# Loads into one of nine ring slots issued as 112 + 8 + 8 partitions in place of 128

## The chip, the cores and the metric

The kernel runs on one core of one Trainium2 chip. The metric is device time in microseconds of one execution. The kernel before has a median of 1238.89 us over three runs (1235.37 to 1240.13).

## The reference

Two layers of a diffusion backbone on 256 latent tokens of width 1024, with 256 context tokens. Layer 0 mixes with latent attention and a pooling mixer and then applies a dense SwiGLU. Layer 1 mixes with a 2-D Fourier transform and then applies eight expert SwiGLUs, of which each token uses two. All is float32.

```python
def swiglu(h, w1, w3, w2):
    return (jax.nn.silu(h @ w1) * (h @ w3)) @ w2

def moe_swiglu(h, router_w, w1, w3, w2):
    logits = (h @ router_w).astype(jnp.float32)
    top_v, top_i = lax.top_k(logits, TOP_K)          # TOP_K = 2 of N_EXPERTS = 8
    top_p = jax.nn.softmax(top_v, axis=-1)
    gates = jnp.sum(jax.nn.one_hot(top_i, N_EXPERTS, dtype=jnp.float32) * top_p[..., None],
                    axis=-2).astype(h.dtype)
    y = jnp.zeros_like(h)
    for e in range(N_EXPERTS):
        y = y + gates[..., e:e + 1] * swiglu(h, w1[e], w3[e], w2[e])
    return y
```

w1 and w3 are 1024 x 3584 for each expert, w2 is 3584 x 1024: 44 MB an expert, 352 MB for the eight.

## The kernel before, in words

SP issues every load, in one fixed order, on one hardware queue (q1 in the profile). Up to about 400 us of the span this is the modulation, mixer and dense weights. From then on it is the experts' weights, and the change lies there.

An expert's weights are cut into 42 pieces of 1 MB, taken as 21 pairs (PAIRS). A pair is 128 rows, one for each partition, of 16 KB (4096 float32). The pairs go through a ring of nine slots (SLOTS = 9) in SBUF: pair number n goes to slot n % 9, and PAIR_PIECE says where in the tensor "held" a slot lies. Pairs 0 to 19 and the last few come as two halves of 1 MB (comes_by_halves, load_half, L680). All others come whole (load, L676), 143 of them in an execution. Before it issues a load into a slot, SP waits for the semaphore e_used, which TensorE raises as it finishes with pieces: expert_loads holds the rule.

Each slot has its own semaphore, piece_in[slot][0], for whole loads and for first halves. A transfer raises it by 16. TensorE waits for 16 times the number of landings expected there. loads_into(slot, lo, hi) counts the loads of a slot in a range of pair numbers, landings adds them up over experts, and the last pair's count is worked out from the same function beside the final down.

Experts are handled in groups of two (GROUP). Each has room for 96 tokens, those at places 1, 5 and 7 only for 64 (LIGHT_PLACES). The matmuls of w1 and w3 are L2398 ("up", N = 256), those of w2 L2413 ("down", N = 512). The matmuls take longer in an expert with 96 places than in one with 64; the bytes loaded are the same. ScalarE and VectorE turn the products in between (L1099, L1761), the results are summed back over tokens by L2367, and L2377 gathers the tokens of the next group.

A second loop over rounds would serve an expert with more tokens than its places; with these inputs it isn't entered. ACT issues eight small table loads (q10) during the experts. The instruction streams of the engines are themselves fetched from memory by DMA (q8 in the profile).

Of the kernel before, what the change touches and what calls it, by code (L numbers as in the profile page):

```python
# [15 lines left out]
P = 128  # L16
# [100 lines left out]
FIRST_LOOP = UNROLLED * GROUP_PAIRS - 1  # L117
SLOTS = 9
ODD_IN_HALF = {3: 1, 8: 0}
BY_HALVES = PAIRS - 1  # L120
END_HALVES = FIRST_LOOP + GROUP_PAIRS - 4
PAIR_AT = {("up", 0, 0): 0, ("up", 0, 1): 2, ("down", 3): 4, ("up", 1, 0): 5, ("up", 1, 1): 7, ("down", 0): 9,
# [97 lines left out]
def build(nc, vec_d, con_d, rope_d, x_d, ctx_d, ada_d, mixa_d, mixb_d, attn_d, mixout_d, ffn_d,  # L220
          dft_d, fnet_d, router_d, moe_d, out_d):
    ctx = ExitStack()
    with ctx:
# [3 lines left out]
        def sem(name):  # L227
            return ctx.enter_context(nc.semaphore(name))
# [25 lines left out]
        def view(t, at, *dims):  # L254

            n = int(np.prod(dims))
            v = t[:, at:at + n]
            if len(dims) == 2:
                return v.rearrange("p (a b) -> p a b", a=dims[0])
            if len(dims) == 3:  # L260
                return v.rearrange("p (a b c) -> p a b c", a=dims[0], b=dims[1])
            return v
# [91 lines left out]
        unit_free = [sem(f"unit_free{i}") for i in range(UNIT_SLOTS)]  # L354
        piece_in = [[sem(f"piece_in{slot}_{s}") for s in range(1 if slot in ODD_IN_HALF else 2)] for slot in range(SLOTS)]
        scratch_free = sem("scratch_free")
# [47 lines left out]
        half_in, half_free = [sem(f"half_in{n}") for n in range(HALF_BUFFERS)], [sem(f"half_free{n}") for n in range(HALF_BUFFERS)]  # L404
        for slot, b in ODD_IN_HALF.items():
            piece_in[slot].append(half_in[b])
        odd_before = [16 * len(range(ODD_IN_HALF[slot], HALVES, HALF_BUFFERS)) if slot in ODD_IN_HALF else 0 for slot in range(SLOTS)]
        sum_ready, scaled_summed = sem("sum_ready"), sem("scaled_summed")
# [52 lines left out]
        def queue_at(i, q):  # L461

            return PAIRS * i + q - 1 if i or q >= AHEAD else q
# [8 lines left out]

        def loads_into(slot, lo, hi):

            return len([n for n in range(lo, hi) if n % SLOTS == slot])

        def landings(group, j, q):

            slot = slot_of_pair(group, j, q)
            if ahead_of_loop(group):  # L480
                return loads_into(slot, 0, queue_at(GROUP * group + j, q) + 1)
            here = loads_into(slot, FIRST_LOOP, FIRST_LOOP + PAIRS * j + q + 1)
            each = loads_into(slot, FIRST_LOOP, FIRST_LOOP + GROUP_PAIRS)
            return each * group + (loads_into(slot, 0, FIRST_LOOP) - UNROLLED * each + here)

        def comes_by_halves(n):

            return n < BY_HALVES or END_HALVES <= n < FIRST_LOOP + GROUP_PAIRS

# [62 lines left out]
        def landed(slot):  # L552

            return view(held, PAIR_PIECE[slot] * PIECE, 2 * PIECE)
# [77 lines left out]
        def _(sp):  # L632
# [37 lines left out]
            def pair_of(e, q):  # L670

                return moe_d[e, 2 * q:2 * q + 2].rearrange("a (m s) c -> (a m) s c", s=2)

            def load(slot, e, q):

                sp.dma_start(landed(slot).rearrange("p (s c) -> p s c", s=2), pair_of(e, q)).then_inc(piece_in[slot][0], 16)  # L676

            def load_half(slot, e, q, s):

# [47 lines left out]
            def expert_loads(e, before, i, group, j):  # L727

                by_halves = [] if ahead_of_loop(group) else [q for q in range(PAIRS) if comes_by_halves(FIRST_LOOP + PAIRS * j + q)]
                for q in range(PAIRS):  # L730
                    if q == 0 and j == 0 and not isinstance(group, int):
                        sp.wait_ge(e_used, PIECES * i - 2)
                    elif (q + PAIRS - SLOTS) % PAIRS not in QUAD_SECOND:
                        sp.wait_ge(e_used, PIECES * i + used_with((q + PAIRS - SLOTS) % PAIRS, 1, q - SLOTS - 1))
                    if q not in by_halves:
                        load(slot_of_pair(group, j, q), before if q == AHEAD else e, q)
                    elif q in QUAD_SECOND:
                        for s in range(2):
                            for d in (1, 0):
                                load_half(slot_of_pair(group, j, q - d), e, q - d, s)  # L740
                    elif q not in QUAD_FIRST:
                        for s in range(2):
                            load_half(slot_of_pair(group, j, q), e, q, s)
# [3 lines left out]
            for (phase, *_), q in PAIR_AT.items():  # L747
                for s, n in ([(s, queue_at(0, q) + d) for s in range(2) for d in range(2)] if phase == "up" else
                             [(s, queue_at(0, q) + d) for d in range(1 if q == AHEAD else 2) for s in range(2)]):
                    if SLOTS <= n < BY_HALVES and q != AHEAD:  # L750
                        left = n - SLOTS
# [1793 lines left out]
```

## Time and profile before

| | |
|---|---|
| median of three runs | 1238.89 us |
| profiled execution, its own time | 1238.51 us |
| its span | 1236.7 us |
| mean granted TensorE clock | 0.991 |
| TensorE busy | 1194.7 us, 97% |
| read from memory | 456.81 MB, 370 GB/s over the span |
| longest queue, q1 | 455.77 MB |

The span is the time from the first to the last recorded instruction. A DMA share of 1.00 means that all sixteen DMA engines of the core are busy; it can read 1.01, because successive packets overlap a little. GB/s is what they moved.

### The profile page before, as it was taken

The page shows a single profiled execution, that of the slowest core. Times are in us where ns is not written, and L with a number is a line of the kernel's source. Part 1 is how long each engine was busy: PE and PEld are TensorE (multiplying, and loading weights), DVE is VectorE, ACT ScalarE, POOL GpSimd, SP SyncE. Part 2 cuts the span into 40 slices and gives each one's busy share as a digit, 9 for nine tenths or more (in the row PEclk, how much of TensorE's full clock was granted, in tenths as well). Part 3 has the DMA queues.
Part 4 walks back from the last instruction along what each step waited for, and adds up shares of the span by engine and source line. Part 5 has one row for each costly group of instructions (what it writes and reads, how often), then busy time and mean ns, then how long its engine had stood idle before and what let it go on. Part 6 is the DMA issues. An engine that isn't in the chain of part 4 may idle for free.

```text
span 1236.7 us, 33565 instructions
## 1 busy us (share of the span) xinstructions
PE 1194.7 (97%) x15501; PEld 775.9 (63%) x15501; DVE 432.6 (35%) x869; ACT 225.6 (18%) x387; POOL 16.6 (1%) x34
## 2 busy tenths in 40 slices
PE   8999999999999999999999999999999989999797
PEld 6767999999997654454655555555545445544454
DVE  4588699999866101021120020103002101101203
ACT  4375543333443000000000000000000000000002
POOL 0400000000000000000000000000000000000000
PEclk9999999999999999999999999999999989999999
DMA  9963699988847899999999999999999999999992
GB/s 390 358 235 112 271 390 356 353 343 329 336 172 294 322 404 387 422 421 425 424 427 425 426 424 427 425 418 400 405 423 424 426 427 425 426 424 427 425 419 116
DMA packets 40270, 460.11 MB, mean 372 GB/s; under 512 B 4672, under 2 KB 5056, under 8 KB 7104
## 3 DMA queue, kind: packets, MB, share of 16 engines
q1 hardware_dynamic: 38784, 455.77, 89.8%
q8 instruction: 123, 2.02, 0.6%
q10 hardware_dynamic: 1344, 2.16, 0.5%
q14 instruction: 19, 0.16, 0.0%
HBM read 456.81 MB, written 1.11 MB: 370 GB/s over the span
## 4 chain that ended last, share of the span: by engine, by line
PE 69%; DVE 14%; DMA 13%; issue 3%; ACT 1%; SPq 0%; DVEq 0%; ACTq 0%
PE bank L2398 37%; PE bank L2413 17%; DMA held<-in_moe 10%; DVE work L1213 6%; DVE split L1197 4%; PE bank L1939 4%; DMA ring<-in_ada 2%; PE bank L2011 1%; PE bank L1831 1%; PE bank L2367 1%; PE bank L2377 1%; DMA ring<-in_fnet 1%; DVE ring L1487 1%; DVE split L1498 1%; PE bank L2147 1%
## 5 line engine op out<-in xcount | busy, mean ns | idle before, releaser
L2398 PE MATMUL bank<-held,work 128*32 128x256 f32 x9408 | 522.8, 383 | 21.9 <-DMA held<-in_moe 11.7
L2398 PEld LDWEIGHTS bank<-held,work 128*32 128x32 f32 x9408 | 315.1, 111 | 235.0 <-issue 49.8
L2413 PE MATMUL bank<-held,moe 128*32 128x512 f32 x2352 | 258.2, 592 | 0.0
L1761 DVE TENSOR_TENSOR moe<-moe,bank 128x256 f32<-128x256 f32 (+1 forms) x84 | 28.2, 385 | 608.7 <-ACT moe L1099 608.7
L2413 PEld LDWEIGHTS bank<-held,moe 128*32 128x32 f32 x2352 | 77.1, 110 | 161.5 <-issue 155.3
L1099 ACT ACTIVATE moe<-bank 128x256 f32<-128x256 f32 (+1 forms) x84 | 24.4, 357 | 737.3 <-PE bank L2398 737.3
L2232 PE MATMUL bank<-split 128*128 128x256 f32 x1024 | 125.4, 283 | 0.9 <-DVE split L1197 0.7
L2232 PEld LDWEIGHTS bank<-split 128*128 128x128 f32 x1024 | 123.8, 191 | 1.7 <-DVE split L1197 1.3
L1197 DVE TENSOR_TENSOR split<-ring,split 128x2048 fp32r<-128x2048 f32 x33 | 75.5, 2290 | 7.4 <-ACT split L992 3.3
L1213 DVE SCALAR_TENSOR_TENSOR work<-ring,condp,work 128x512 f32<-128x512 f32 x98 | 73.7, 752 | 4.1
L992 ACT ACTIVATE split<-ring 128x2048 fp32r<-128x2048 f32 x31 | 59.4, 1915 | 74.9 <-PE bank L2232 72.6
L2222 PE MATMUL bank<-split 128*128 128x256 f32 x480 | 59.4, 283 | 0.0
L2222 PEld LDWEIGHTS bank<-split 128*128 128x128 f32 x480 | 58.3, 192 | 0.4 <-issue 0.4
L1939 PE MATMUL bank<-split 128*128 128x256 f32 x384 | 47.5, 284 | 0.0
L1939 PEld LDWEIGHTS bank<-split 128*128 128x128 f32 x384 | 46.4, 190 | 1.4 <-issue 1.4
L1747 DVE SCALAR_TENSOR_TENSOR xT<-bank,ada,xT 128x256 f32<-128x256 f32 x64 | 25.9, 476 | 54.3 <-PE bank L2377 54.3
L1152 DVE TENSOR_TENSOR split<-ring,split 128x1024 fp32r<-128x1024 f32 (+1 forms) x24 | 27.8, 1176 | 7.5 <-ACT split L837 7.2
L837 ACT ACTIVATE split<-ring 128x1024 fp32r<-128x1024 f32 (+1 forms) x24 | 24.0, 1018 | 33.4 <-PE bank L1939 18.2
L1765 DVE STREAM_TRANSPOSE moe<-moe 128x256 f32<-128x256 f32 (+1 forms) x84 | 28.2, 384 | 0.0
L2011 PE MATMUL bank<-split 128*128 128x256 f32 x168 | 25.8, 305 | 1.1 <-ACT split L866 0.9
L2011 PEld LDWEIGHTS bank<-split 128*128 128x128 f32 x168 | 21.6, 190 | 4.0 <-issue 3.5
L1739 DVE SCALAR_TENSOR_TENSOR split<-bank,small,split 128x512 fp32r<-128x512 f32 x16 | 11.3, 747 | 32.3 <-ACT split L1074 32.3
(277 smaller groups left out, 640.7 us busy)
## 6 DMA issues: line engine op xcount, KB each, us to landing
held<-in_moe SPq DMA_DIRECT2D x143, 2048.0 KB, 27.7
held<-in_moe SPq DMA_DIRECT2D x50, 1024.0 KB, 9.7
ring<-in_ffn SPq DMA_DIRECT2D x16, 2048.0 KB, 8.4
ring<-in_ada SPq DMA_DIRECT2D x28, 1024.0 KB, 6.9
ring<-in_ada SPq DMA_DIRECT2D x10, 2048.0 KB, 10.1
ring<-in_mixout SPq DMA_DIRECT2D x2, 2048.0 KB, 8.8
ring<-in_fnet SPq DMA_DIRECT2D x2, 2048.0 KB, 9.9
ring<-in_mixa SPq DMA_DIRECT2D x2, 1024.0 KB, 15.2
```

The costliest lines, as they stand in the source:

```text
L992: nc.scalar.activation(high_d[:, q % SPLITS_DENSE, :], piece_view(q), ACT.Copy).then_inc(high_ready, 1)
L1152: nc.vector.tensor_tensor(mixer_part(m, 1), mixer_source(m), plain(mixer_part(m, 0)), ALU.subtract).then_inc(mixer_low, 1)
L1197: nc.vector.tensor_tensor(low_d[:, q % SPLITS_DENSE, :], piece_view(q), plain(high_d[:, q % SPLITS_DENSE, :]), ALU.subtract).then_inc(low_ ...
L1213: ins = nc.vector.scalar_tensor_tensor(out=total, in0=half_view(h)[:, k, :], scalar=weight, in1=total, op0=ALU.mult, op1=ALU.add)
L1761: nc.vector.tensor_tensor(gate_e[:, g, 0:n], gate_e[:, g, 0:n], bank[g][:, n:2 * n], ALU.mult).then_inc(e_hidden, counts_for(light, g))
L1765: nc.vector.transpose(hiddenT[phase % 2][:, g, 0:n].rearrange("p (a s r) -> p a s r", s=2, r=QUAD), gate_e[:, g, 0:n].rearrange("p (a r s) ...
L1939: last = mm(bank[banks[c // 2]][:, (c % 2) * T:(c % 2) * T + T], parts[left][:, k, j * P:(j + 1) * P], source[right][:, k0 + k, :], start= ...
L2011: last = mm(out, parts[left][:, k, lo:hi], h_in[right][:, k0 + k, 0:n], start=((left, right) == PRODUCTS[0] and k0 + k == 0 and opens), st ...
L2222: last = mm(bank[FFN_BANKS[k // 2]][:, (k % 2) * T:(k % 2) * T + T], w[:, j, k * P:(k + 1) * P], hidden_parts[g % 2][:, right, j, :], star ...
L2232: last = mm(bank[kind == "w3"][:, j * T:(j + 1) * T], w[:, k, j * P:(j + 1) * P], h_parts[:, right, k, :], start=(n == 0 and j == 0 and k ...
L2398: last = mm(out[:, :, block, :].rearrange("p z (a r) -> p z a r", a=2), x_group[:, 4 * s + k, j * CAP + g * QUAD:j * CAP + (g + 1) * QUAD] ...
L2413: last = mm(bank[3 + n][c * QUAD:(c + 1) * QUAD, :], hiddenT[phase % 2][:, g, blk * QUAD:(blk + 1) * QUAD], weights[:, s, j, n * 512:(n + ...
```

## The change

The whole loads into slot 4 are issued as three transfers, of partitions 0 to 111, 112 to 119 and 120 to 127, in place of one of 128. All three raise the slot's semaphore by 16, so that such a load counts three landings, and a load by halves still one. Bytes, places and order are the same.

```diff
+TILTED_SLOT, TILTED_ROWS = 4, ((0, 112), (112, 120), (120, 128))
...
         def loads_into(slot, lo, hi):
 
-            return len([n for n in range(lo, hi) if n % SLOTS == slot])
+            each = len(TILTED_ROWS) if slot == TILTED_SLOT else 1
+            return sum(1 if comes_by_halves(n) else each for n in range(lo, hi) if n % SLOTS == slot)
...
             def load(slot, e, q):
 
-                sp.dma_start(landed(slot).rearrange("p (s c) -> p s c", s=2), pair_of(e, q)).then_inc(piece_in[slot][0], 16)
+                for lo, hi in TILTED_ROWS if slot == TILTED_SLOT else ((0, P),):
+                    sp.dma_start(landed(slot)[lo:hi].rearrange("p (s c) -> p s c", s=2), pair_of(e, q)[lo:hi]).then_inc(piece_in[slot][0], 16)
```

On SP, where the first whole loads stand (an ISA row computes the address in memory), before:

```order
L676 ISA
L676 DMA held<-in_moe 128x4096
L676 ISA [waits e_used]
L676 DMA held<-in_moe 128x4096
L676 ISA
L676 DMA held<-in_moe 128x4096
```

and the same place now:

```order
L679 ISA
L679 DMA held<-in_moe 128x4096
L679 ISA [waits e_used]
L679 DMA held<-in_moe 128x4096
L679 ISA
L679 DMA held<-in_moe 112x4096
L679 ISA
L679 DMA held<-in_moe 8x4096
L679 ISA
L679 DMA held<-in_moe 8x4096
```

The third whole load is pair 22, the first for slot 4 that comes whole. It has become three transfers, each with its address instruction, and none waits for anything of its own. The same happens at every ninth load, 16 times on the path that runs.

## Rows read from the trace of the kernel before

**Rows 1.** The page's head and part 1: busy time of each engine.

```profile
span 1236.7 us, 33565 instructions
PE 1194.7 (97%) x15501; PEld 775.9 (63%) x15501; DVE 432.6 (35%) x869; ACT 225.6 (18%) x387; POOL 16.6 (1%) x34
```

**Rows 2.** Stretches of the expert stage: busy of each engine, clock, DMA share, GB/s.

```profile
core 0: us, PE busy (x) PEld busy (x) DVE busy (x) ACT busy (x) POOL busy (x), PEclk, DMA share, GB/s
500.00:820.00 320.00, 315.90 (x4744) 169.05 (x4740) 42.49 (x124) 15.99 (x46) 0.00 (x0) 0.99 1.01 425
820.00:910.00 90.00, 90.00 (x1412) 46.99 (x1408) 12.21 (x34) 4.07 (x11) 0.00 (x0) 1.00 0.99 406
910.00:1190.00 280.00, 265.34 (x3929) 138.13 (x3924) 37.75 (x110) 13.04 (x37) 0.00 (x0) 0.98 1.01 425
```

**Rows 3.** Waits of PE after 500 us: total, times, longest.

```profile
PE bank L2398 <- DMA held<-in_moe: 11.7, 6, 5.6
PE bank L2398 <- issue: 9.2, 2, 6.1
```

**Rows 4.** PE in order of time, 955 to 1225 us: start, length, instructions, idle before.

```profile
992.82 7.56 PE L2398 MATMUL bank<-held,work 128*32 128x256 f32 x85 [6.09 <-issue]
...
1173.42 16.92 PE L2398 MATMUL bank<-held,work 128*32 128x256 f32 x256 [5.59 <-DMA held<-in_moe]
...
1202.97 3.66 PE L2398 MATMUL bank<-held,work 128*32 128x256 f32 x64 [1.09 <-DMA held<-in_moe]
1206.56 4.20 PE L2367 MATMUL bank<-work_r,split 128*128 128x256 f32 x32
1210.69 10.51 PE L2413 MATMUL bank<-held,moe 128*32 128x512 f32 x96
```

**Rows 5.** The chain that ended last, 500 to 1237 us: start and length.

```profile
558.24 30.42 DMA held<-in_moe
...
1166.46 36.37 DMA held<-in_moe
```

**Rows 6.** DMA queues between 505 and 1195 us: packets, MB, share of sixteen engines.

```profile
q1 hardware_dynamic: 20044, 288.40, 98.9%
q8 instruction: 79, 1.29, 0.8%
```

**Rows 7.** Two-microsecond stretches at the end of the stream, columns as in rows 2.

```profile
1205.00:1207.00 2.00, 2.00 (x35) 1.29 (x28) 0.00 (x0) 0.24 (x2) 0.00 (x0) 1.00 0.99 414
1207.00:1209.00 2.00, 2.00 (x19) 2.00 (x18) 0.94 (x4) 0.44 (x3) 0.00 (x0) 1.00 0.65 266
1209.00:1211.00 2.00, 2.00 (x18) 1.63 (x20) 0.95 (x3) 1.23 (x4) 0.00 (x0) 1.00 0.51 209
1211.00:1213.00 2.00, 2.00 (x24) 0.65 (x20) 0.54 (x2) 0.00 (x0) 0.00 (x0) 1.00 0.53 221
1213.00:1215.00 2.00, 2.00 (x24) 0.52 (x16) 0.00 (x0) 0.00 (x0) 0.00 (x0) 1.00 0.47 197
1215.00:1217.00 2.00, 2.00 (x24) 0.65 (x20) 0.00 (x0) 0.00 (x0) 0.00 (x0) 1.00 0.21 82
1217.00:1219.00 2.00, 2.00 (x24) 0.52 (x16) 0.00 (x0) 0.00 (x0) 0.00 (x0) 1.00 0.05 20
1219.00:1221.00 2.00, 2.00 (x24) 0.49 (x16) 0.00 (x0) 0.00 (x0) 0.00 (x0) 1.00 0.03 8
```

**Rows 8.** SP's issues, 502 to 820 and 1160 to 1237 us: ns min/median/max, landing.

```profile
L676 SPq DMA_DIRECT2D held<-in_moe x64: 332/333/1122, 502.6 to 813.6; - x64
DMA to landing us min/median/max: 12.9/28.0/37.9
...
L680 SPq DMA_DIRECT2D held<-in_moe x10: 332/334/4572, 1164.9 to 1196.3; - x10
```

**Rows 9.** The stretch after the long wait, and one of half loads; columns as before.

```profile
1178.00:1190.00 12.00, 12.00 (x216) 7.66 (x212) 0.00 (x0) 0.00 (x0) 0.00 (x0) 0.95 1.00 421
1194.00:1206.00 12.00, 9.90 (x153) 5.23 (x149) 0.00 (x0) 0.00 (x0) 0.00 (x0) 1.00 1.02 422
```

**Rows 10.** DMA issues: count, KB each, median us from issue to landing.

```profile
vec<-in_vec SPq DMA_DIRECT2D x1, 79.5 KB, 2.0
```

## The prediction

> **What bounds the kernel now.** I read the page's busy shares first, then the stretches of the expert stage, then the DMA queues, then what PE waits for, and last the end of the weight stream. TensorE is busy 97% of the span and the other engines at most 35% [rows 1]; that alone would call this a TensorE kernel. The stretches say that it has two bounds. From 500 us on the sixteen DMA engines are busy with a share of 1.00 or 1.01 and move 425 GB/s, except between 820 and 910 us, where they fall to 0.99 and 406 GB/s while PE never pauses [rows 2]. So the experts with 96 places make the stream wait for PE around 820 to 910, and the experts with 64 places make PE wait for the stream: all PE waits for held after 500 us sum to 11.7 us under DMA and 9.2 us that the view calls issue [rows 3]. The longest of them lie in two places, 6.09 us before 992.8 and 5.59 us before 1173.4, and after that every short wait up to 1203 ends with a landing [rows 4]. From 1202.97 PE runs through without a real pause until the tail (3.66, 4.20 and 10.51 us). What releases it at 1202.97 is a landing 36.37 us after issue [rows 5]. At the end the weight stream sets the time.
>
> Which part of the stream? A transfer has landed when its slowest DMA engine is done. The queue rows show a second traffic on the same engines: instruction fetches, 79 packets of 1.29 MB, 16 KB each, between 505 and 1195 us, with 0.8% of sixteen engines' time [rows 6]. That is 0.008 x 16 x 690 = 88 engine-us, 1.1 us each, against 16,384 B / (425/16 GB/s) = 0.62 us for one row of 16 KB of weights. The end of the stream shows that this load isn't spread evenly [rows 7]. Until 1207 the share is 0.99. Then it is 0.65, and 0.51, 0.53, 0.47: half of the engines have nothing left and the other half still work. 0.21, 0.05 and 0.03 follow, so the last one ends near 1218.6. The area behind 1207 is 2.45 x 2 us x 16 = 78 engine-us; less 5 for the first eight's remainder it leaves 73, that is 9 us for each of the late eight, with the latest at about 11. The first eight also stood dry between 820 and 910: 0.02 x 90 x 16 = 29 engine-us, 3.6 us each. So in 700 us the late eight did 9 + 3.6 = 12.6 us more than the others. If only eight engines carry the fetches, these give them 88/8 = 11 us each. The sums agree within the rounding, so I take it that eight engines of the sixteen carry all the fetches, never run dry, and set every late landing. The trace doesn't number the engines.
>
> **The change.** It removes nothing. Slot 4 takes every ninth load; of the loads that come whole, 16 are for slot 4 (32 in the program's text, of which 16 stand in the loop for further rounds, which doesn't run here). Each becomes 112 + 8 + 8 rows.
>
> Rows per engine. Of 128 rows each of sixteen engines carries 8. Of 112 each carries 7, if they are spread evenly. Eight rows keep at most eight engines at work, one row each. If both small transfers take the same eight, these carry 9 rows and the others 7. That moves 0.62 us of work per load: over 16 loads +9.9 us on one eight and -9.9 us on the other. No row of before shows a transfer on fewer than sixteen engines; by the nearest rows the bounds are 8 against 8 (the two transfers take different eights: nothing changes) and 9 against 7. I take 9 against 7, because both small transfers have the same shape and come from the same queue. The Trainium skill (DMA: Bandwidth & Descriptors, on why a DMA increments its semaphore by 16) says a transfer uses the largest number of engines up to 16 that divides its rows, and that on this path these are the lowest-numbered. By it 9 against 7 is certain, and the heavy eight are engines 0 to 7; no row here shows it, and it doesn't say which engines fetch instructions.
>
> Everything now hangs on which eight gets the ninth row.
>
> If it is the early eight: the late eight lose 9.9 us and the last of them ends at 1218.6 - 9.9 = 1208.7. The early eight ended between 1207 and about 1209.4 [rows 7], and get 9.9 us more. But they stood dry for 3.6 us, and this goes first: seven of the 16 loads fall before 820 us (64 whole loads up to there, every ninth [rows 8]), so they arrive at that place 4.3 us later than before and find work. Net 9.9 - 3.6 = 6.3 us: they end at 1209.4 + 6.3 = 1215.7. The last landing moves from 1218.6 to 1215.7, 2.9 us earlier, and so does the one at 1202.8, after which PE has nothing but its own work. Bounds: nothing of the dry time is used, 1209.4 + 9.9 = 1219.3, 0.7 us later; all is used and PE, which gets its data earlier from 559 us on, also frees slots earlier, up to 4 us earlier.
>
> The other edits. SP issues 32 transfers more at 0.33 us each [rows 8]: 11 us on SP in all, hidden because a load lies 28 us in the queue before it lands. What is queued behind them on SP are the next loads, which are late only if the queue is empty; it is full from 500 us on. SP is held up itself at 1166 to 1188, up to 4.57 us for one issue [rows 8], that is, with a full queue; more entries may hold it there longer, and a full queue starves nobody. The cost of a transfer inside the stream: the last ten loads are halves of 1 MB, twice as many transfers for the same bytes, and run at 422 GB/s against 425 [rows 9]. 3/425 of 12 us is 0.08 us for two to three more transfers, at most 0.04 us each, or 1.3 us over 32; the lower bound is 0, since the rate rounds. I take 0.2 us. The semaphore counts 48 for such a load, and PE waits for all three parts: nothing on PE moves.
>
> The Trainium skill (same page, rules for kernel authors) speaks against the change: it advises one transfer of 128 partitions over two for disjoint parts, since the parts share the same engines and serialize, and to keep each at 1 MiB or more. For halves of a full load the trace disagrees: 422 beside 425 GB/s. At 128 KB no run here shows it yet; what it would do is the third rival.
>
> Sum: -2.9 + 0.2 = -2.7 us. The profiled execution has a span of 1236.7 and a time of 1238.51, 0.4 below the median of 1238.89. From the median: 1236.2.
>
> **The rivals.**
> 1. The ninth row falls on engines that also fetch: on all of them, or on some, which costs the same because a landing waits for the slowest. For it: the trace can't name the fetching engines, and if they were chosen at random most choices would touch the heavy eight. Against it: the fetchers are exactly eight, which looks like one half of the sixteen, and then it is one half or the other. Price: those engines never run dry, so nothing absorbs it. The late engines end 9.9 us later, the lag at the end grows from 11 to 21 us, and from 559 us on PE waits for it. 1238.9 + 9.9 = 1249, up to 1252 if the longer pauses draw TensorE down to 1.2 GHz more often: the granted clock is already 0.95 in the stretch after the long wait at 1173 [rows 4, 9]. This decides from the first fetching engine that gets a ninth row. It is my slower case.
> 2. No tilt: the two small transfers take different eights, or the rows are shared in another way. Then only the 32 issues are left: 1239.
> 3. Small transfers break the stream: each costs its own start and end rather than lying in the queue. For it: a transfer of 79.5 KB alone takes 2.0 us to land [rows 10]. 32 x 2.0 = 64 us if all of it shows, and some 6 us if a tenth does. Against it: the queue holds 28 us of work, and the halves cost nothing to speak of. Place it at 1245.
> 4. The stream gives back more than I count: PE's waits of 20.9 us after 500 us shrink by half. It would need the early eight to have more room than the dry 3.6 us. 1230.
>
> **How the numbers follow.** Forecast (fetchers are the light eight, over-corrected a little): 0.60, at 1236.2, own range 1233 to 1240. Rival 1: 0.26, 1246 to 1252. Rival 2: 0.06. Rival 3: 0.04. Rival 4: 0.04. Half a per cent, 6.2 us, is about what a measurement of this kernel can tell from no change. Faster: rival 4 and a few parts of the forecast, 0.07. Slower: rivals 1 and 3 but for a remainder, 0.28. Same: 0.65. The range must reach into rival 1: 1233 to 1250.
>
> **What would show it.** Forecast right: at the end of the stream the share no longer stays near 0.5 for 6 us behind one edge; the wait before 1173 and those behind it shrink by 2 to 3 us in all; between 820 and 910 the rate rises from 406 towards 415 GB/s. Rival 1: the half-empty stretch grows towards 20 us, PE's waits for held grow by some 10 us. Rival 2: the half-empty stretch is unchanged. Rival 3: the rate inside 910 to 1190 drops below 420 without any engine waiting. The forecast is wrong if the fetches don't explain the late half at all; then the lag would not answer to rows moved between engines.

## The result, and the profile after

The changed kernel takes 1452.14 us, median of six runs (1443.81 to 1459.02), beside 1236.6 us of the kernel before in six runs. The ratio is 1.1728 [1.1707, 1.1748]: 215.5 us, or 17%, slower. The forecast was 1236.2 us, and its range ended at 1250. One ring slot of nine, 16 loads of 2 MB, is all that was cut differently; that makes 215.5 / 16 = 13.5 us for each of these loads, where a whole load takes 2.097 MB / 425 GB/s = 4.9 us.

The page's head of the kernel after answers to [rows 1], with the rows of the weight loads from the DMA part (count, KB each, us to landing):

```profile
span 1449.1 us, 33665 instructions
PE 1248.6 (86%) x15501; PEld 806.1 (56%) x15501; DVE 432.6 (30%) x869; ACT 225.3 (16%) x387; POOL 17.0 (1%) x34
...
held<-in_moe SPq DMA_DIRECT2D x127, 2048.0 KB, 46.4
...
held<-in_moe SPq DMA_DIRECT2D x16, 1792.0 KB
```

PE has the same 15,501 matmuls, but is busy 53.9 us longer. The number of loads is as meant: 127 whole and 16 of 112 rows (1792 KB). A whole load now takes 46.4 us from issue to landing in the median.

What PE waited for after 500 us (total, times, longest) answers to [rows 3]:

```profile
PE bank L2401 <- DMA held<-in_moe: 105.0, 24, 9.6
PE bank L2401 <- issue: 69.5, 15, 10.5
PE bank L2416 <- DMA held<-in_moe: 4.6, 2, 3.7
PE bank L2416 <- issue: 2.1, 1, 2.1
```

L2401 is the line that was L2398. Together 181.2 us, where [rows 3] had 20.9: 160.3 us more of waiting for weights. With the 53.9 us more of busy time that is 214 us, and the span grew by 212.4. So the whole difference is accounted for by TensorE waiting for the weight stream and by its longer busy time at a lower clock around these waits.

PE in order of time at its last wait for a load, and the first hold in the chain of waits behind 525 us:

```profile
1415.70 3.66 PE L2401 MATMUL bank<-held,work 128*32 128x256 f32 x64 [1.19 <-DMA held<-in_moe]
```

```profile
526.30 32.91 DMA held<-in_moe
```

The last wait for a landing ends at 1415.70, where [rows 4] had it at 1202.97: 212.7 us later, the whole of the difference. Behind it nothing changed. The chain leaves PE for the stream 32 us earlier than [rows 5] did (there 30.42 us from 558.24, here 32.91 us from 526.30), and then does so much more often: 50.5% of it from 500 us on are landings, where it was 17.0%.

The stretches of [rows 2] (columns as there: busy of the engines, granted clock, DMA share, GB/s):

```profile
500.00:820.00 320.00, 266.48 (x3772) 140.92 (x3768) 37.81 (x108) 12.97 (x36) 0.00 (x0) 0.91 1.01 343
820.00:910.00 90.00, 74.15 (x1020) 40.66 (x1012) 4.87 (x16) 3.01 (x10) 0.00 (x0) 0.92 0.99 322
910.00:1190.00 280.00, 214.12 (x2904) 118.52 (x2908) 26.96 (x78) 9.84 (x28) 0.00 (x0) 0.90 0.94 320
```

The share of the DMA engines is what it was in the first two stretches (1.01, 0.99) and a little lower in the third (0.94 beside 1.01), but they move 343, 322 and 320 GB/s in place of 425, 406 and 425. Apart from some places in the third stretch (a share of 0.44 from 979 to 987 us) the engines don't stand still: they are busy and slow. That reading is the key to the case, and it gets sharper when the stretches follow the loads of slot 4, here the second to the fourth of them:

```profile
500.00:527.00 27.00, 27.00 (x444) 14.89 (x437) 3.06 (x7) 1.92 (x4) 0.00 (x0) 1.00 1.01 426
528.00:544.00 16.00, 14.08 (x194) 6.14 (x192) 5.51 (x18) 0.66 (x2) 0.00 (x0) 1.00 1.00 228
545.00:579.00 34.00, 22.77 (x324) 12.51 (x328) 1.45 (x4) 0.66 (x2) 0.00 (x0) 0.86 1.00 425
580.00:598.00 18.00, 15.90 (x184) 9.39 (x176) 2.43 (x8) 1.91 (x6) 0.00 (x0) 0.91 1.00 216
600.00:631.00 31.00, 26.58 (x392) 14.58 (x388) 0.00 (x0) 0.00 (x0) 0.00 (x0) 0.83 1.01 426
632.00:657.00 25.00, 17.08 (x252) 10.12 (x244) 8.12 (x22) 2.20 (x5) 0.00 (x0) 0.96 1.01 224
```

At each of these loads the stream falls from 425 to between 216 and 228 GB/s for 16 to 25 us with all sixteen engines busy, then it is whole again. Each of the three stretches loses nearly half of its length: (1 - 228/425) x 16 = 7.4 us, and 8.9 and 11.8 us. The granted clock of TensorE is lower behind pauses of PE: 0.86 and 0.83, a mean over stretches at its two levels of 1.2 and 2.4 GHz.

### The profile page after: what moved, and what is told of

Same layout as the page of the kernel before. It is cut to its first block, busy times and chain, and to the rows that moved or that the text cites. A ratio compares the mean times of both kernels' runs of the same rounds, so it can differ in the third digit from the quotient of the medians.

```text
span 1449.1 us, 33665 instructions
## 1 busy us (share of the span) xinstructions
PE 1248.6 (86%) x15501; PEld 806.1 (56%) x15501; DVE 432.6 (30%) x869; ACT 225.3 (16%) x387; POOL 17.0 (1%) x34
## 4 chain that ended last, share of the span: by engine, by line
PE 45%; DMA 34%; DVE 12%; issue 4%; another core or an unknown queue 2%; ACT 1%; SPq 1%; DVEq 0%; ACTq 0%
DMA held<-in_moe 33%; PE bank L2401 25%; PE bank L2416 8%; DVE work L1216 5%; DVE split L1200 4%; PE bank L1942 3%; DMA ring<-in_mixa 1%; PE bank L2014 1%; PE bank L1834 1%; PE bank L2380 1%; DVE ring L1490 0%; PE bank L2370 0%; DVE split L1501 0%; PE bank L2150 0%
## 5 line engine op out<-in xcount | busy, mean ns | idle before, releaser
L2401 PE MATMUL bank<-held,work 128*32 128x256 f32 x9408 | 569.6, 405 | 175.5 <-DMA held<-in_moe 105.0
L2401 PEld LDWEIGHTS bank<-held,work 128*32 128x32 f32 x9408 | 342.4, 117 | 411.1 <-issue 246.1
L2416 PE MATMUL bank<-held,moe 128*32 128x512 f32 x2352 | 263.3, 599 | 6.7 <-DMA held<-in_moe 4.6
L2416 PEld LDWEIGHTS bank<-held,moe 128*32 128x32 f32 x2352 | 81.3, 111 | 168.8 <-issue 156.1
L1942 PEld LDWEIGHTS bank<-split 128*128 128x128 f32 x384 | 46.4, 190 | 1.4 <-issue 1.4
L2370 PE MATMUL bank<-work_r,split 128*128 128x256 f32 x160 | 21.5, 288 | 1.1 <-DVE work_r L1653 0.8
## 6 DMA issues: line engine op xcount, KB each, us to landing
held<-in_moe SPq DMA_DIRECT2D x127, 2048.0 KB, 46.4
```

What stands on the lines that cost most here:

```text
L1942: last = mm(bank[banks[c // 2]][:, (c % 2) * T:(c % 2) * T + T], parts[left][:, k, j * P:(j + 1) * P], source[right][:, k0 + k, :], start= ...
L2401: last = mm(out[:, :, block, :].rearrange("p z (a r) -> p z a r", a=2), x_group[:, 4 * s + k, j * CAP + g * QUAD:j * CAP + (g + 1) * QUAD] ...
L2416: last = mm(bank[3 + n][c * QUAD:(c + 1) * QUAD, :], hiddenT[phase % 2][:, g, blk * QUAD:(blk + 1) * QUAD], weights[:, s, j, n * 512:(n + ...
```

## The experiments

In the kernels that change only slot 4, the row pairs became pairs of a row and a column slice, and each cut below shows the line that names them; the load itself then reads

```
for rows, cols in TILTED_ROWS if slot == TILTED_SLOT else ((slice(0, P), slice(0, 2 * PIECE)),):
    sp.dma_start(landed(slot)[rows, cols], pair_of(e, q).rearrange("p s c -> p (s c)")[rows, cols]).then_inc(piece_in[slot][0], 16)
```

Five kernels (shapes, stream, stream with fetches and the two on fetches) hold nothing of the reference: SP's loads alone, or loads beside small matmuls that serve only to have instructions fetched. Each of the five is known from one run.

### Shapes by themselves

Loads only, eight of each shape, one shape after another, the next stage when the last has landed:

```
-sp.dma_start(slot(n)[0:128], pair(n)[0:128])                # stage 1
+sp.dma_start(slot(n)[0:112], ...); [112:120]; [120:128]     # stage 2, and so on
```

> A kernel with nothing but weight loads: fourteen stages of eight loads, each stage issued back to back and waited for, nothing computed (the output is not the reference's). It tells which shape of transfer is slow. Port theory (engines of one transfer write to the same port of SBUF when it isn't of 128 rows): 128 rows 420 GB/s; 112 alone and 64 + 64 about half, 200 to 250; 112 + 8 + 8 about 2 MB in 13 to 14 us, 150 GB/s; eight neighbouring rows 54 GB/s, eight rows four apart 200 GB/s; copies within memory, which touch no SBUF, run equally fast with 112 and with 128 rows; stores of 112 rows are as slow as loads of 112. Tilt theory (only the count of rows per engine matters): 112 alone 420, 112 + 8 + 8 is 8/9 of 420, 375; both eight-row forms 200. Per-transfer theory (each transfer costs a fixed time): 112 alone 420, 112 + 16 and 64 + 64 equal, one fixed cost above 128. Memory-side theory: copies of 112 rows within memory are half as fast as those of 128.

Measured, one stretch within each stage; the last three columns are clock, DMA share and GB/s:

```profile
2.50:42.50 40.00, 0.00 (x0) 1.00 0.97 412
45.00:125.00 80.00, 0.00 (x0) 1.00 0.91 206
128.00:184.00 56.00, 0.00 (x0) 1.00 0.98 255
187.00:254.00 67.00, 0.00 (x0) 1.00 0.99 244
258.00:336.00 78.00, 0.00 (x0) 1.00 1.00 209
340.00:379.00 39.00, 0.00 (x0) 1.00 0.98 419
382.00:454.00 72.00, 0.00 (x0) 1.00 0.99 228
457.00:474.00 17.00, 0.00 (x0) 1.00 0.43 46
478.00:484.00 6.00, 0.00 (x0) 1.00 0.38 137
487.00:525.00 38.00, 0.00 (x0) 1.00 0.99 421
528.00:573.00 45.00, 0.00 (x0) 1.00 0.89 309
577.00:626.00 49.00, 0.00 (x0) 1.00 0.96 321
629.00:672.00 43.00, 0.00 (x0) 1.00 0.96 320
```

In order: 128 rows, 412 GB/s. 112 + 8 + 8 rows, 206. 112 alone, 255. 112 + 16, 244. 64 + 64, 209. Every other row, even and then odd, 419. 96 + 32, 228. Eight neighbouring rows, 46; eight rows four apart, 137. Stores of 128 rows, 421, and of 112 rows, 309. Copies from memory to memory of 128 and 112 rows, 321 and 320. A fourteenth stage, seven whole loads and one in three parts, ran at 362.

So a transfer of 112 rows costs more time than one of 128, though it carries fewer bytes (8 x 1.835 MB / 255 GB/s = 58 us beside 41). The two small ones aren't needed for that. Two transfers of 64 rows each run at full rate if they take every other row, and at half of it if each takes one half of the partitions. And where neither side is on-chip memory, 112 rows run as fast as 128 (a fall to 255 would have shown below 321). What counts is which partitions a transfer touches, on the on-chip side. The first of the expectation's four theories had 112 alone and 64 + 64 right (200 to 250), but 112 + 8 + 8 too low (150 for 206), stores of 112 rows too slow (as slow as loads, for 309), and eight rows four apart too fast (200 for 137).

The Trainium skill gives a reason for most of this (SBUF — State Buffer, section "Door 1: The DMA port swizzle"): the on-chip memory is reached by sixteen ports of eight partitions each, bits 2 to 4 and 6 of the partition's number pick the port, and the bandwidth depends on how many ports the partitions reach. For these shapes the trace agrees: by that map a half of 64 partitions reaches eight ports (209 GB/s), every other row all sixteen (419); eight neighbouring rows from 112 on reach two, eight rows four apart reach eight (46 and 137; that last stage is only 9 us long and paced by SP's issues of 0.62 us, and in the long stages below the same shape runs at 195 and 209).

The records of the single packets say the same more directly. A packet with one row of 16 KB takes 0.61 us in the median in the stages of 128 rows, of even and odd rows, and of eight rows four apart. It takes 1.27 us in 64 + 64, about twice as long, and 2.41 us in eight neighbouring rows, four times as long: as if two and four engines shared a port. The same map doesn't explain the shape of this case by the number of ports alone: 112 rows still reach all sixteen, and run at 255 GB/s, with 1.01 us a packet. That engines meet at the same ports at the same time is the likely reading there; the trace names neither engines nor ports, so it is argued and not shown.

### Who carries the fetches, and does it matter?

Loads of eight rows each (every fourth row of 32), first alone, then beside matmuls that have instructions fetched. The first kernel keeps eight such loads in flight; the second keeps four, with 32 KB in a row in place of 16:

```
+sp.dma_start(slot(n % 8)[0:32:4], pair(n)[0:32:4])                    # first
+sp.dma_start(held[0:32:4, n % 4 * 2 * WIDE:...], flat[32 * n:32 * n + 32]...)  # second
```

> Two stages of 320 transfers of eight rows four apart, eight in flight, the first with TensorE idle, the second with 3200 small matmuls beside them, which need some 25 instruction fetches; nothing of the reference is computed. It tells which engines fetch. If the fetches ride on the eight engines that carry eight-row transfers, the second stage is 2 to 4% longer than the first (25 x 1.1 us / 8 = 3.4 us of 200) and the share of the sixteen engines stays at 0.50. If they ride on the other eight, the second stage is as long as the first and the share rises to 0.51 to 0.52. Mixed: in between.

> Experiment 2 again with rows of 32 KB (256 KB a transfer), so that the eight engines and not SP set the pace: two stages of 160 transfers of eight rows four apart, four in flight; TensorE idle in the first, running small matmuls in the second, with an instruction fetch every 7 us (nothing of the reference is computed). If none of the fetching engines is among the eight (the prediction's forecast): both stages equally long, about 196 us, within 1. If all or some are (rival 1): each of them gets a fetch every 57 us, which costs it 1.1 to 1.6 us, and the second stage is 4 to 6 us longer.

Both stages of the first kernel, then both of the second:

```profile
5.00:215.00 210.00, 0.00 (x0) 0.00 (x0) 0.00 (x0) 1.00 0.50 195
225.00:420.00 195.00, 195.00 (x3496) 195.00 (x3494) 0.00 (x0) 1.00 0.51 195
```

```profile
5.00:200.00 195.00, 0.00 (x0) 0.00 (x0) 0.00 (x0) 1.00 0.50 209
210.00:410.00 200.00, 200.00 (x3585) 200.00 (x3583) 0.00 (x0) 1.00 0.50 201
```

In the first kernel the rate is 195 GB/s with and without fetches. By the words of its expectation this speaks for the other eight engines, but the test had no force: SP takes 0.62 us for each issue and hardly ever waits for a landing (7.0 us in all), so SP sets the pace and an engine that loses 1 us catches up unseen. It did show that a transfer of eight rows keeps half of the engines busy (share 0.50), as the prediction took it. In the second the rate falls from 209 to 201 GB/s, and the stage grows from 204 to 213 us. The rate alone would be weak evidence, since it also drifts from 212 to 204 GB/s between the halves of the first stage. The single packets decide. Eight row packets are under way at any time; during the fetches number 3, 4, 11, 12, 19, 20, 27 and 28 of the second stage it is seven for practically the whole length of the fetch (0.88 to 1.02 us), and during the others eight for most or all of it. So two of every eight fetches that follow each other stop one of the row-carrying engines, and six fall on engines that carry no rows. The period of eight fits fetches that go round eight engines, of which two are in the half that the small transfers use. The prediction's premise, that the fetching engines are exactly the other half, was wrong; its first rival ("on some") was right. By the prediction's own price that is worth some 10 us, not 215.

### The tilt taken away

```
-TILTED_SLOT, TILTED_ROWS = 4, ((0, 112), (112, 120), (120, 128))
+TILTED_SLOT, TILTED_ROWS = 4, ((slice(0, 112), slice(0, 4096)), (slice(112, 128), slice(0, 4096)),)
```

> The changed kernel with 112 + 16 rows in place of 112 + 8 + 8: every engine carries 7 + 1 rows, so no tilt. Tilt theory (rival 1 of the prediction): the loss is gone, 1237. Port theory: most of the loss stays, since the 112 rows are as badly spread as before: +80 to +200 us. Per-transfer theory: one extra transfer in place of two, half the loss, +107.

Measured: 1426.43 us, ratio 1.1524 [1.1496, 1.1551], that is +189 us or 11.8 a load. By the prediction's count sixteen rows share out evenly over sixteen engines; there is no ninth row on anyone, and nearly nine tenths of the loss stay. Its stretches at the third and the fourth load of slot 4 have the same form as those of the changed kernel:

```profile
582.00:596.00 14.00, 14.00 (x176) 8.96 (x171) 2.43 (x8) 1.92 (x6) 0.00 (x0) 0.91 1.00 242
632.00:649.00 17.00, 15.20 (x232) 8.81 (x224) 5.16 (x13) 1.27 (x2) 0.00 (x0) 1.00 1.00 214
```

### Three transfers, but all of 128 rows; two of every other row

```
+TILTED_ROWS = ((slice(0, 128), slice(0, 3584)), (slice(0, 128), slice(3584, 3840)), (slice(0, 128), slice(3840, 4096)))   # by columns
+TILTED_ROWS = ((slice(0, 128, 2), slice(0, 4096)), (slice(1, 128, 2), slice(0, 4096)),)                                   # even, odd rows
```

> The loads into slot 4 come as three transfers again, but of all 128 rows, cut by columns into 14, 1 and 1 KB of each row. As many transfers as in the changed kernel, no tilt, the row shape of before. Per-transfer theory: the loss stays, +215 us. Port and tilt theory: 1237, within 5 us.

> The loads into slot 4 as two transfers of 64 rows, the even and the odd partitions. Rows are split as in the changed kernel, each engine carries 4 + 4, but the rows of one transfer spread over all ports; by themselves they ran at 412 GB/s. Port theory: 1237, within 5 us. A theory by which any cut of the partition axis costs (fewer rows than 128 in a transfer): at least the 190 us of 112 + 16.

Measured: by columns, in the same sizes of 1792, 128 and 128 KB, 1239.94 us, ratio 1.0014 [1.0003, 1.0025]; even and odd rows 1236.36 us, 1.0001 [0.9986, 1.0017]. The 32 more issues, the small size of the transfers and the higher counts of the semaphores cost 1.7 us in all by the ratio, with 0.4 and 3.1 as its bounds (the prediction had 0.2), and cutting a load by rows costs nothing if each part still reaches over all partitions. The third rival, small transfers that break the stream, falls with the first of these.

### The tilt without the shape

Five transfers by rows, so that by the prediction's count eight engines carry nine rows, with every part spread out:

```
+TILTED_ROWS = (0:128:2), (1:128:4), (3:64:4), (67:96:4), (99:128:4)     # first
+TILTED_ROWS = (0:128:2), (1:128:4), (3:32:4), (35:64:4), (67:128:4)     # second
```

> The tilt of the prediction, 9 rows on the engines that carry eight-row transfers against 7 on the others, made of rows that lie apart: 64 even rows, 32 rows of every fourth, 16 rows and twice 8 rows four apart. Five transfers in place of three. Tilt by rival 1 (some of the fetching engines among the heavy eight): +9.9 us, 1247. Tilt by the forecast (all fetchers among the light eight): -3 us, 1234. Port theory adds little: only the 16 rows put two engines on a port, one row each, 0.6 us a load if all of it shows, so 1240 to 1257 together with rival 1. If the tilt itself makes the loss, 1450.

> The tilt of 9 against 7 rows of experiment 6, cut otherwise: 64 even rows, 32 of every fourth, and the eight-row transfers lie in partitions 0 to 63, on the ports that the same engines serve in a load of 128 rows; the 16 rows left lie in 64 to 127. If the 72 us of experiment 6 came from engines that write to ports which others serve at the time: here only the 16 rows do, and the loss falls to less than half, 1237 + 10 to 35. If it comes from the tilt or from five transfers in place of one: as before, 1309.

Measured: the first 1309.14 us, ratio 1.0602 [1.0578, 1.0626], +72; the second 1264.81 us, 1.022 [1.020, 1.024], +27. The first missed every expectation that stood for it; the second fell inside its 10 to 35. Both have the same number of transfers and the same tilt; they differ only in where the last three transfers go: the two of eight rows above partition 64 and the one of sixteen below it, or the other way round. The stretch at the second load of slot 4, of the first kernel and then of the second:

```profile
527.00:534.00 7.00, 7.00 (x118) 4.72 (x120) 4.53 (x14) 0.00 (x0) 0.00 (x0) 1.00 1.00 266
```

```profile
525.00:532.00 7.00, 7.00 (x112) 4.70 (x104) 4.53 (x14) 0.00 (x0) 0.00 (x0) 1.00 1.01 336
```

So 45 us hang on nothing but which partitions these 32 rows of a load go to. The second expectation had a reading for it: the loss comes from rows that one engine writes where another engine is writing at the time, and the second kernel has fewer of them. Its number came true; the reading itself stays argued, since the trace doesn't number the engines. The prediction's tilt, together with five transfers in place of one, shows here as no more than the second kernel's 27 us.

### The dose

An eighth of the bytes of each load in the bad shape, the rest whole:

```
+TILTED_ROWS = ((slice(0, 128), slice(0, 3584)), (slice(0, 112), slice(3584, 4096)), (slice(112, 120), ...), (slice(120, 128), ...))
```

> The loads into slot 4 with 14 KB of each row in one transfer of 128 rows, and only the last 2 KB of each row as 112 + 8 + 8 rows. If the loss goes by the bytes in the badly spread shape: 1/8 of 215, +27 us, 1264. If it goes by the number of such transfers or by the meeting of shapes as such: most of the 215. If a short badly spread transfer is hidden: 1237.

Measured: 1264.21 us, ratio 1.0216 [1.0199, 1.0233], +26.5 us. That is 215.5 / 26.5 = 8.1 times less for 8 times fewer bytes. The loss goes with the bytes that are moved in the shape, and not with the number of such transfers.

### Why 13 us a load, when the shape alone costs 4.5

All 143 whole loads as 112 + 16, and a stream of loads alone with a ring of eight slots:

```
-each = len(TILTED_ROWS) if slot == TILTED_SLOT else 1
+each = len(TILTED_ROWS)
```

> Every whole load, 143, as 112 + 16 rows. If a load costs by its own shape only, as when all are alike (8.7 us against 5.1, experiment 1): 143 x 3.6 = +515 us, about 1750, where 16 of them cost 190 (11.9 each). If each costs what one costs among whole ones, 143 x 11.9 = +1700, about 2940. The first says that most of the loss at one in nine comes from the meeting of the two shapes in the queues, the second that a load costs 11.9 us by itself.

> Nothing but loads, eight slots in a ring, four stages of 63 loads: all whole; one in nine as 112 + 8 + 8; one in nine as 112 + 16; one in nine as even and odd rows. TensorE is idle and there are no instruction fetches of it (output not the reference's). All whole: 63 x 4.92 = 310 us. If the loss of the kernel is the loss of the stream alone: seven loads x 13.5 = +94 us for 112 + 8 + 8 and 7 x 11.9 = +83 for 112 + 16. If PE's waits, its clock and the lag by fetches multiply it: 7 x 5 to 6.4 = +35 to +45 and 7 x 3.6 = +25. Even and odd: +0 to +3.

Measured: all loads in two parts 1890.71 us (one run), +653.8 or 4.57 us for each of 143 loads. That is above the 3.6 of the expectation's first case and far below the 11.9 of its second. A load costs less than half of what one in nine costs (11.8). The steady rate, and the four stages of the stream alone (all whole; one in nine as 112 + 8 + 8; one in nine as 112 + 16; one in nine as even and odd rows), with two stretches of the second stage, at an odd load and behind it:

```profile
700.00:1700.00 1000.00, 610.29 (x7796) 309.31 (x7800) 69.60 (x204) 25.38 (x74) 0.00 (x0) 0.80 1.01 220
```

```profile
1.50:311.00 309.50, 0.00 (x0) 1.00 1.01 427
313.00:687.00 374.00, 0.00 (x0) 1.00 0.99 353
689.00:1030.00 341.00, 0.00 (x0) 1.00 1.00 387
1032.00:1342.00 310.00, 0.00 (x0) 1.00 1.00 426
330.00:350.00 20.00, 0.00 (x0) 1.00 1.01 294
350.00:380.00 30.00, 0.00 (x0) 1.00 1.01 428
```

By the starts of SP's issues the first three stages last 311.3, 376.1 and 343.0 us. In a clean stream the seven odd loads cost 376.1 - 311.3 = 64.8 us (9.3 a load) in three parts, and 343.0 - 311.3 = 31.7 us (4.5) in two; even and odd rows cost nothing. Three parts lie between the two cases of the expectation (5 to 6.4 and 13.5 a load), two parts a little above the lower one (3.6). So 4.5 of the 11.8 us of the kernel without tilt are the shape, and the rest needs something that the stream alone doesn't have. Instruction fetches were the candidate.

The same stream with matmuls beside it that have instructions fetched: stage 1 one in nine as 112 + 16 without fetches, stage 2 all whole with fetches, stage 3 both.

```
+for n in range(7600): nc.tensor.matmul(bank[0:32, 0:64], tile[:, 0:32], tile[:, 64:128], ...)   # on PE, stages 2 and 3
```

> The load-only ring of experiment 7: a stage of 63 loads with one in nine as 112 + 16, TensorE idle; then, with small matmuls on TensorE and so a fetch every 7 us, a stage of 63 whole loads and one with 112 + 16 again (nothing of the reference is computed). First stage 343 us, as before. Whole loads with fetches: 311 + 6 to 10. Theory that fetches put the engines out of step and so lengthen the stretches in which two shapes meet: the last stage loses clearly more per load than the first, 7 to 12 us against 4.5, so 360 to 395. Theory that the additional loss in the kernel comes from PE's waits and SP's: the last stage is as the first plus what the whole loads gained, 350.

Measured: the three stages, then a stretch of stage 1 and four of stage 3 (the first, second, fourth and sixth of its seven), each at an odd load:

```profile
0.00:345.00 345.00, 0.00 (x0) 0.00 (x0) 0.41 (x5) 1.00 1.00 383
347.00:667.00 320.00, 320.00 (x5702) 320.00 (x5699) 0.00 (x0) 1.00 0.98 415
667.00:1028.00 361.00, 340.05 (x6018) 337.79 (x6016) 0.00 (x0) 1.00 1.01 344
120.00:130.00 10.00, 0.00 (x0) 0.00 (x0) 0.00 (x0) 1.00 0.98 233
689.00:702.00 13.00, 12.23 (x219) 12.07 (x217) 0.00 (x0) 1.00 0.99 228
739.00:755.00 16.00, 15.32 (x274) 15.16 (x273) 0.00 (x0) 1.00 1.00 213
844.00:866.00 22.00, 18.52 (x329) 18.20 (x326) 0.00 (x0) 1.00 1.00 208
956.00:981.00 25.00, 20.97 (x373) 20.65 (x371) 0.00 (x0) 1.00 1.01 216
```

By SP's issues the stages last 345.7, 320.1 and 399.3 us. Against the clean 311.3 us of the kernel before (the stage that both kernels have differs by 2.7 us between them) the shape alone costs 34.4, the fetches alone 8.8, and both 88.0: 45 us more than their sum. Without fetches every stretch at half rate is 10 to 11 us long; with them they grow at first from load to load, 13, 16, 18 and 22 us, and then stay at 25 or 26. In the changed kernel they are 12, 16, 18, 25 and 20 us at the first five loads. Per odd load stage 3 costs (399.3 - 320.1) / 7 = 11.3 us beside stage 2, and the kernel with the same cut 11.8. So the size of the loss comes back without PE's waits and without any load that waits for PE. (Fetches are denser here, one in 7.3 us, than in the changed kernel, one in 11.5.)

How the two make each other worse was not measured by itself. The likely reading is that fetches put some engines behind the others, so that different engines are at the odd load at different times, and the meeting of the two shapes lasts longer. Two things in the traces speak for it. The first is the end of a stage, where no load follows and an engine that is ahead falls idle. These are the ends of the second stage (112 + 8 + 8) and the third (112 + 16) of the stream alone, and then of the three stages of the last kernel:

```profile
680.00:684.00 4.00, 0.00 (x0) 1.00 0.53 225
1023.00:1027.00 4.00, 0.00 (x0) 1.00 1.02 434
340.00:344.00 4.00, 0.00 (x0) 0.00 (x0) 0.00 (x0) 1.00 0.94 401
658.00:662.00 4.00, 4.00 (x76) 4.00 (x74) 0.00 (x0) 1.00 0.54 229
1054.00:1058.00 4.00, 4.00 (x75) 4.00 (x73) 0.00 (x0) 1.00 0.45 188
```

With 112 + 16 and no fetches the engines end almost together: the share is still 1.02 when 4 us are left, and 0.94 when 2 us are left. With the tilt, or with fetches, only about half of the engines are at work from 8 or 9 us before the end, and with the shape and fetches together the share is 0.45 already 12 us before it. The second is the distance from one odd load to the next by SP's issues. From the second odd load on it is 44.05 us for even and odd rows. For 112 + 16 it stays at 48.7 to 49.0 us in the first stage of the last kernel, without fetches, and in its third stage, with them, it grows from 54.0 over 54.9, 56.8 and 58.6 to 60.1. For 112 + 8 + 8 without fetches, where the tilt alone can drive the engines apart, it grows too, from 52.0 to 54.4.

## Why the prediction was wrong

**The step that failed is "The cost of a transfer inside the stream"**, with "Rows per engine" ahead of it. It priced the parts by bytes per engine, at 8, 7 or 9 rows of 0.62 us, and bounded the rest by the halves of 1 MB at 422 GB/s [rows 9]. Those halves are cut by columns: each still has 128 rows. The trace of before held no transfer of fewer rows in the stream, and the bounds should have said so. The term was 0.2 us; the runs show 1.7 us for the number and size of the transfers (three by columns) and some 189 of the 215 us for the shape of 112 and 16 rows, tilt excluded and what the fetches add to it included.

**Ninth row.** "Eight rows keep at most eight engines at work" holds (share 0.50). So does nine rows against seven: at the end of the clean stream with 112 + 8 + 8 half of the engines fall idle some 10 us early (share 0.53 at 680 to 684), where seven loads at two rows of 0.62 us make 8.7, and with 112 + 16 they don't. That the fetching engines are the light eight does not hold: two of them are in the heavy half. The gain of 2.9 us at the end of the stream never had a chance to show. From the kernel with 112 + 16 to that with 112 + 8 + 8 the time rises by 26 us, and the clean stream has 4.8 us a load for it (9.3 - 4.5); two narrow transfers of neighbouring rows are themselves slow (46 GB/s). So even this part is not chiefly the ±0.62 us a load of the prediction.

**What bounds the kernel** was read rightly, and it is why the loss shows in full: the stream sets the time from 500 us to its end, PE already waited 20.9 us for it, and so every microsecond that the stream lost came out at the end (212.7 at the last landing). The premise that a queue of 28 us hides small things holds for issue times, which are latency; it doesn't hide a loss of rate.

**The rule that was set aside.** The Trainium skill's advice (DMA: Bandwidth & Descriptors, "Rules for kernel authors") against two transfers for disjoint parts was set aside because halves at 422 GB/s disagreed. The halves weren't disjoint in partitions, so they said nothing on it. The Trainium skill's section "Can I just issue two DMAs to hit both halves?" (SBUF — State Buffer) says that the ports are picked from a single transfer's span, and that only one transfer over all 128 partitions reaches all sixteen. For two halves the trace agrees (209 GB/s). For the even and odd rows it limits that: two transfers of 64 rows each, which both span nearly all 128 partitions, ran at 419 GB/s.

**The rivals.** The slower one had the right sign and the wrong cause (its "on some" was true). The third had the right sign to look for, "the rate inside 910 to 1190 drops below 420 without any engine waiting": it came as 320 GB/s, at a share of 0.94 and with PE waiting. But its cause was the size of a transfer, it was placed at 1245 with 4 in 100, and its upper end of 64 us was not carried into the range. No case had a mechanism that can reach 215 us. That one of the listed signs came true is luck, and no merit of that rival.

**The clock.** PE is busy 53.9 us longer. The long waits are followed by stretches at a lower grant (0.86 and 0.83 above), as the prediction said for the stretch after 1173. With all loads in two parts it was 0.80 over a whole millisecond. What the lower clock adds to the time of the kernel was not measured by itself; the stream beside fetches loses nearly the same for each odd load (11.3 and 11.8 us) with no load that waits for PE, so it is not needed for the loss.

## What to carry to other kernels

Before a transfer is cut, ask which partitions each part touches, not only how many bytes and engines it gets: parts by columns, or every other row, kept 422 to 425 GB/s, and parts by blocks of rows ran at about half of it. A bound taken from the nearest row holds only if that row has the same shape in the dimension that changes; if none has, the range must say so. And one odd transfer in nine can slow its neighbours: look for stretches where the DMA share is 1.0 and the GB/s are half.

## What the runs showed of the hardware

- 112 rows took longer than 128 (255 GB/s beside 412, so 7.2 us beside 5.1 a load), though they are fewer bytes on the same sixteen engines; stores of 112 rows ran at 309 beside 421 GB/s.
- One packet of a 16 KB row took 0.61 us where the partitions were spread, 1.27 us in halves of 64 neighbouring rows and 2.41 us in eight neighbouring rows.
- The same odd load (112 + 16 rows) cost 4.5 us in a clean stream and 11.3 us beside instruction fetches, though the fetches alone cost 8.8 us in 320. That engines out of step are the reason is the likely reading, and not shown by itself.
- Instruction fetches stopped a row-carrying engine in two of every eight cases (8 of the first 28 in the second stage of the kernel with rows of 32 KB). That fits fetches that go round eight of the sixteen DMA engines, two of which are among the eight that carry transfers of eight rows.
